# Last layer's expert rows by one-hot products on chip, and a ninth slot in the ring of expert weights with a quarter of the descriptors' scratch

## The reference, cut to what matters

```python
def swiglu(x, w_gu, w_down):
    g, u = jnp.split(x @ w_gu, 2, axis=-1)
    return (jax.nn.silu(g) * u) @ w_down

# moe_ffn(h, ...), h (N, D)
scores = jax.nn.sigmoid(jnp.dot(h, router_w, preferred_element_type=jnp.float32))
_, idx = lax.top_k(scores + router_bias.astype(jnp.float32), TOP_K)      # TOP_K = 6 of 64
gates = jnp.take_along_axis(scores, idx, axis=-1)
gates = gates / jnp.sum(gates, axis=-1, keepdims=True) * ROUTED_SCALE    # 2.5
...
y_rows = lax.map(expert_block, ...)        # swiglu(h[src], w_gu[e], w_down[e]) * gate
routed = jax.ops.segment_sum(y_rows.reshape(n_rows, d), src, num_segments=n_tok + 1)[:n_tok]
return routed + swiglu(h, shared_gu, shared_down)
```

## Time and profile before

| | us |
|---|---|
| median of three runs | 2591.6 |
| lowest and highest run | 2590.67, 2595.17 |
| span of the profiled execution | 2591.4 |
| TensorE busy in it (share) | 2249.8 (87%) |
| DVE busy | 740.5 (29%) |
| ScalarE busy | 417.0 (16%) |
| POOL busy | 311.3 (12%) |
| moved by DMA | 780.92 MB, of it 740.46 by the SP queue |

### The profile page before, as it was taken

One profiled execution on the slowest core, in us unless ns is written; L12 is line 12 of the kernel. 1 busy time (PEld: TensorE's weight loads), 2 busy tenths in 40 slices (PEclk: granted clock), 3 DMA queues, 4 the chain that ended last, 5 costly groups with the idle time before them and its releaser, 6 DMA issues. The chain is left out here.

```text
span 2591.4 us, 40524 instructions
## 1 busy us (share of the span) xinstructions
PE 2249.8 (87%) x17039; PEld 1151.1 (44%) x17039; DVE 740.5 (29%) x1653; ACT 417.0 (16%) x886; POOL 311.3 (12%) x368
## 2 busy tenths in 40 slices
PE   6999899999778797888888999898978889888887
PEld 2457644454333343434434557655433334343333
DVE  2365655371011011111115466645201101011112
ACT  2322344110000000000001333431000000000000
POOL 0007200011111111110000007100111101000000
PEclk8999999999989999999999999999998999999999
DMA  8000297279999999999988100136999999999994
GB/s 326 33 17 35 92 377 291 115 286 394 426 424 406 421 409 419 417 416 383 397 356 343 41 31 6 71 117 259 373 426 414 417 415 421 417 418 412 416 419 198
DMA packets 96345, 780.92 MB, mean 301 GB/s; under 512 B 21736, under 2 KB 22136, under 8 KB 37280
## 3 DMA queue, kind: packets, MB, share of 16 engines
q1 hardware_dynamic: 74848, 740.46, 69.7%
q0 software_dynamic: 21312, 37.81, 3.9%
HBM read 772.55 MB, written 41.29 MB: 314 GB/s over the span
## 5 line engine op out<-in xcount | busy, mean ns | idle before, releaser
L1513 PE MATMUL banks<-arena,htreg 128*32 128x384 f32 (+2 forms) x5824 | 879.4, 533 | 199.6 <-DMA arena<-in_exp_w_gu 194.3
L1513 PEld LDWEIGHTS banks<-arena,htreg 128*32 128x32 f32 (+2 forms) x5824 | 403.4, 137 | 648.7 <-issue 507.3
L1538 PE MATMUL banks<-arena,modreg 128*32 128x512 f32 (+2 forms) x2184 | 400.0, 598 | 40.5 <-issue 37.8
L2314 DVE TENSOR_TENSOR modreg<-modreg,banks 128x384 f32<-128x384 f32 x74 | 40.9, 553 | 1029.8 <-ACT modreg L1831 1029.8
L1538 PEld LDWEIGHTS banks<-arena,modreg 128*32 128x32 f32 (+2 forms) x2184 | 137.6, 127 | 250.4 <-issue 247.8
L1064 PE MATMUL banks<-arena,htreg 128*128 128x512 f32 (+3 forms) x480 | 159.0, 490 | 0.0
L2466 DVE COPY modreg<-banks 128x512 f32<-128x512 f32 x68 | 47.0, 691 | 318.9 <-PE banks L1538 318.9
L1837 ACT ACTIVATE modreg<-banks 128x384 f32<-128x384 f32 x74 | 36.3, 490 | 550.5 <-PE banks L1529 550.5
L2629 POOL DMA_INDIRECT y_d<-modreg,lst x68 | 67.5, 992 | 455.4 <-DVE modreg L2466 454.5
L1064 PEld LDWEIGHTS banks<-arena,htreg 128*128 128x128 f32 x480 | 89.7, 191 | 65.0 <-issue 61.0
L1831 ACT ACTIVATE modreg<-banks 128x384 f32<-128x384 f32 x74 | 36.3, 490 | 491.5 <-PE banks L1513 491.5
(11 more groups left out here) (407 smaller groups left out, 2173.6 us busy)
## 6 DMA issues: line engine op xcount, KB each, us to landing
arena<-in_exp_w_gu SPq DMA_DIRECT2D x256, 1536.0 KB
arena<-in_exp_w_down SPq DMA_DIRECT2D x128, 1536.0 KB
arena<-in_w_mod SPq DMA_DIRECT2D x32, 1024.0 KB, 11.4
arena<-y_d SPq DMA_DIRECT2D x6, 3072.0 KB, 16.7
modreg<-in_w_mod SPq DMA_DIRECT2D x14, 1024.0 KB, 8.3
modreg<-mod_d SPq DMA_DIRECT2D x20, 512.0 KB
arena<-in_shared_w_gu SPq DMA_DIRECT2D x6, 1536.0 KB
arena<-in_w_in SPq DMA_DIRECT2D x4, 2048.0 KB, 12.5
```

Of the source, the lines that this page charges most:

```text
L1513: last = mm(gu_bank(n, half)[rows, 0:DE], src[:, k, rows], up4[q][:, i, DE * half:DE * (half + 1)], start=(k == 0), stop=(k == KD - 1))
L1538: last = mm(ps[4 + half][rows, :], actT[:, k, rows], dn3[q][:, k, 512 * half:512 * half + 512], start=(k == 0), stop=(k == KE - 1))
L2314: tt(act_, sgb, gu_bank(n, 1)[:, 0:DE], ALU.mult).then_inc(unit_act.sem, 1)
```

## The change

The routed part of the last layer is written anew; layer 0 keeps its code but for the ring.

- `SLOTS` goes from 8 to 9 and the arena from 27648 to 30720 words; the room is that of the scratch for the software queue's descriptors, `dynamic_dma_scratch_size=4096` instead of the default of 16384 bytes for each partition. Both layers use the ninth slot.
- In layer 1 the units are 25 and not 34: 4 with one expert (128 slots), 4 of an expert with 96 and one with 32, 8 of two experts with 64 each, and 9 of four experts with 32 each ("quads"). The order is quad, whole, pair four times, then quad, big, pair four times, and a last quad. With the two shared units there are 27. The chunks are as many as before (195).
- The rows of a unit are gathered on chip: DVE makes a one-hot matrix `hot` from the token's place in the expert, and TensorE multiplies `h` by it, 16 products of 128 columns in the place of eight transposes. `h_d` is still stored.
- The rows are combined on chip: TensorE picks the gates of the unit's experts (`gate_rows`, 4 products), DVE turns them into a gated one-hot matrix (`gates_of`), TensorE multiplies it by the unit's outputs (`combine`, 4 products of 512 columns) and DVE adds the result (`added`) to `acc_last`. Nothing is scattered to `y_d` or read back; POOL has no work in the stage.
- The expert order comes from a permutation matrix and one product (`order_of_experts`) and not from eight rounds of max, and is complete when it is there.
- The output is stored in four pieces instead of two. In the last unit the modulation's gate is multiplied in ahead of the combining product.
- The overflow path of layer 1 (`more_last`) does its own listings, gathers and scatters, if it is entered.
- A table of 333 words for each partition is loaded in layer 1's mixer. Signals of the routing are put together on fewer semaphores. The cleared list in DRAM grows from 145 to 160 KB.

The diff, cut to its core:

```diff
-WHOLE = (4, 4)
-BIG = (12, 12)
+LAST = DEPTH - 1
+WHOLE = (4,) * LAST
+BIG = (12,) * LAST
-SLOTS = 8
-LIST1 = P * max(UNITS)
+SLOTS = 9
+LIST1 = P * NE
...
+def last_columns():
+    whole = [[(u, i) for i in range(4)] for u in range(4)]
+    big = [[(u, 0), (u, 1), (u, 2), (67 - u, 0)] for u in range(4, 8)]
+    pair = [[(r, 0), (r, 1), (r + 1, 0), (r + 1, 1)] for r in range(8, 24, 2)]
+    quad = [[(r + i, 0) for i in range(4)] for r in range(24, 60, 4)]
+    return whole + big + pair + quad
...
-        A_WORDS = 27648
+        A_WORDS = 30720
...
+        def last_work():
+            units = {kind: [u for u in range(N_LAST) if KIND_OF[u] == kind] for kind in range(4)}
+            order = []
+            for i, quad in enumerate(units[3]):
+                order.append(quad)
+                if i < 4:
+                    order += [units[0][i], units[2][i]]
+                elif i < 8:
+                    order += [units[1][i - 4], units[2][i]]
+            return [(u, tuple(dict.fromkeys(r for r, _ in COLUMNS[u]))) for u in order]
...
# SP
-                        if n == ROUTED_AT[l][FIRST]:
+                        if l < LAST and n == ROUTED_AT[l][FIRST]:
                             sp.wait_ge(sorted_ready.sem, sorted_ready.at(l, 2))
...
# TensorE
+                def order_of_experts():
+                    pe.wait_ge(order_made.sem, order_made.after(LAST, "perm"))
+                    mm(ps[0][0:1, P:P + N_COL], T_("index")[0:NE], perm, start=True, stop=True).then_inc(order_psum.sem, 1)
+                    pe.wait_ge(order_act.sem, order_act.after(LAST, "marks"))
+                    for j in range(2):
+                        last = mm(ps[3][:, N_COL * j:N_COL * j + N_COL], by_expert[:, P * j:P * j + P], perm, start=True, stop=True)
+                    last.then_inc(order_psum.sem, 1)
...
+                def gather_by_product(n):
+                    r = n - EARLY
...
+                    pe.wait_ge(slot_hot_ready.sem, slot_hot_ready.at(LAST, r + 1))
+                    for k in range(KD):
+                        for j in range(2):
+                            rows = h[:, 2 + j, :].rearrange("p (d k) -> p k d", k=KD)
+                            last = mm(ps[k // 4][:, tok(k % 4)], rows[:, k, :], hot[r % 2][:, j, :], start=(j == 0), stop=(j == 1))
+                    last.then_inc(slotT_psum.sem, 1)
+                def gate_rows(n):
+                    u = WORK[l][n][0]
...
+                    for i in range(4):
+                        column = perm[:, 4 * u + i:4 * u + i + 1].broadcast_to([NE, 32])
+                        last = mm(gu_bank(n, 0)[32 * i:32 * i + 32, :], column, by_expert, start=True, stop=True)
+                    last.then_inc(gate_psum.sem, 1)
...
+                def combine(n, j):
...
+                    for half in range(2):
+                        if j and n < NW[l] - 1:
+                            pe.wait_ge(comb_added.sem, comb_added.at(0, 4 * r + half + 1))
+                        mm(comb_bank(n, j, half), gated[r % 2][:, P * j:P * j + P], outs[r % 2][:, 512 * half:512 * half + 512],
+                           start=True, stop=True).then_inc(comb_psum.sem, 1)
...
+                    for n in range(EARLY, NW[l] + 1):
+                        if n < NW[l]:
+                            unit_part(n, "lo")
+                        act_transposed(n - 1)
+                        if n > EARLY:
+                            gate_rows(n - 1)
+                        if n < NW[l]:
+                            unit_part(n, "hi")
+                        if n >= EARLY + 2:
+                            combine(n - 2, 0)
+                        if n + 1 < NW[l]:
+                            gather_by_product(n + 1)
+                        if n >= EARLY + 2:
+                            combine(n - 2, 1)
+                        unit_down(n - 1)
+                    for j in range(2):
+                        combine(NW[l] - 1, j)
...
# DVE
+                    def one_hot(n):
+                        r, u = n - EARLY, WORK[l][n][0]
+                        if r >= 2:
+                            dve.wait_ge(slotT_psum.sem, slotT_psum.at(l, r - 1))
+                        tt(hot[r % 2].rearrange("p t (c s) -> p t c s", s=32), bc(places[:, :, 4 * u:4 * u + 4], 3, 32),
+                           bc(bc(K("slot_no")[:, 0:32], 1, 4), 1, 2), ALU.is_equal).then_inc(slot_hot_ready.sem, 1)
...
+                    for n in range(EARLY, NW[l] + 1):
+                        if n > EARLY:
+                            gates_of(n - 1)
+                        if n < NW[l]:
+                            unit_times(n)
+                        if n >= EARLY + 2:
+                            added(n - 2, 0)
+                        if n + 1 < NW[l]:
+                            unit_copied(n + 1)
+                        if n >= EARLY + 2:
+                            added(n - 2, 1)
+                        if n < NW[l]:
+                            unit_out(n - 1)
+                        if n + 2 < NW[l]:
+                            one_hot(n + 2)
+                        if n == EARLY:
+                            overflow_addresses()
...
-    nc = bacc.Bacc("TRN2", target_bir_lowering=False, num_devices=1)
+    nc = bacc.Bacc("TRN2", target_bir_lowering=False, num_devices=1, dynamic_dma_scratch_size=4096)
```

More of the change, by code:

```diff
@@ L369, in build @@
         RING = 4
-        eid = sb("eid", [P, NE], U32)
+        eid = sb("eid", [P, max(NE, N_COL)], U32)
         lst1 = sb("lst1", [P, max(UNITS)], U32)
@@ new lines, in _ @@
+                dve.wait_ge(h_ready.sem, h_ready.at(2 * l + 1, n_t))
+                link(dve.memset(mask[:, n_t, :], 0.0))
+                dve.wait_ge(order_act.sem, order_act.after(l, "scores"))
+                link(tt(selb[:, nt_, :], scores[:, nt_, :], bc(srow("rbias"), 1, n_t), ALU.add))
+                for i in range(n_t):
+                    link(dve.max(out=top8[:, i, :], in_=selb[:, i, :]))
+                    link(dve.max_index(out=idx8[:, i, :], in_max=top8[:, i, :], in_values=selb[:, i, :]))
```

568 lines of the change are left out of this document (395 added, 173 removed).

## The result

The kernel after takes 2536.7 us (median of four runs, 2532.6 to 2537.6) against 2593.1 (four runs) for the kernel before on the same chip: a ratio of 0.978, 95% interval 0.977 to 0.979. The forecast was 2511 us with a range of 2494 to 2536. The direction holds; that the weights' transfers bound the last layer's expert stage throughout does not, and 26 us of the 81 that were expected aren't there.

The account below looks back on a forecast made before the run. Weight transfers were taken to bound the expert stages. Last landing 2497.2, less 3 for layer 0, plus 7 for the last down product and 9.2 for the end, gave 2510.4; 0.2 more, say 2511 us; range 2494 to 2536.

Parts of the forecast that it names:

- Loads before the ring: Last layer's expert loads: first chunk at 1766.8, the SP queue's 18.0 us wait for the expert order goes, none replaces it.
- Rows and pitch: Last layer's expert stage: row traffic goes, 192 chunks at 3.77 us each take 723.8 us.
- rival 3: Expert transfers: no lag, queue at 426 GB/s, 3.70 us a chunk, 13 us less, layer 0 gains 4: 2494; chance 0.12.
- The lag of 5 us: End of the last layer's weight transfers: some DMA engines finish late; 5 us kept, ends 0 and 10.
- TensorE: Last-layer units: 25.1 us each with a 4.4 us gather; 75.4 us a group against 79.2 of weights, cover 3.8.
- Rival 1: Last layer's first groups: TensorE becomes the bound; at 6.1 us a gather 16 us more, 2527; chance 0.20.
- The ninth slot: Layer 0's ring: one more chunk held ahead of each shared unit saves 3 us, between 0 and 8.
- Rival 2: Last layer's ring: nine slots don't carry quads, the queue starves for 16 us, 2529; chance 0.12.
- The scratch: Layer 0's software-queue descriptors: a quarter of the scratch costs nothing, between 0 and rival 5's price.
- rival 5: Layer 0: small scratch makes POOL wait for the previous DMA's landing, 192 us dearer, 2703; chance 0.05.
- Rival 4: Last layer: rows were hidden, chunk pitch stays 3.87 to 4.0; at 3.96 landing 37 us later, 2548; chance 0.06.
- The end: After the last landing: 7 us for the last down product, then 9.2 for gating, combining, add, handovers and store.

Follow-up runs that it names:

- e1: Kernel after with the gather reading neighbouring words of h instead of every eighth (features mixed, same amount of work): 2499.9 us, 0.9635 of the kernel before.
- e2: Kernel after with half of the gather's products left out, stride kept: 2497.9 us, ratio 0.9635.
- e6: Kernel after, whole computation, VectorE writing the last layer's h in gather order and gate/up weights laid out to match: 2502.5 us, ratio 0.9653.
- e11: e6 plus software-queue copies on POOL, DRAM to DRAM, 128 rows of 4 KB for each of 24 last-layer units, never read: 2526.2 us, ratio 0.975.
- e12: e11 with each copy written in 256 pieces of 2048 bytes with a gap behind each, same bytes: 2524.0 us, ratio 0.975.
- e3: Kernel before with nine slots and the small descriptor scratch, one semaphore of the output's stores spared: 2583.9 us, ratio 0.9968.
- e4: Kernel before with only the small descriptor scratch (4096 bytes): 2592.7 us against 2591.8, ratio 1.0001.
- e5: Kernel after with eight ring slots instead of nine: 2574.2 us, ratio 0.992.
- e8: e6 with eight ring slots instead of nine: 2521.7 us, ratio 0.974.
- e7: Kernel after with the gather's weight loads reading every second word instead of every eighth (features mixed): 2500.2 us, ratio 0.965.
- e10: Kernel after with the gather's weight loads reading every fourth word instead of every eighth (features mixed): 2535.8 us, ratio 0.978.
- e9: Kernel after, whole computation, gather on neighbouring words, last-layer lo/hi weight chunks loaded in matching order as 3072-byte pieces: 2513.4 us, ratio 0.970.

## Why the prediction was right or wrong

The sum and what it met, in the trace of the kernel after:

| term | forecast | after |
|---|---|---|
| first expert issue | 1763.8 | 1763.05 |
| from there to the last landing | 730.4 | 751 |
| to the end of the last down product | 7 | 10 |
| end | 9.2 | 11.7 |
| sum | 2510.4 | 2535.7 |

**What bounds the kernel before** was read rightly, by the windows of share 1.00 with TensorE idle in between. e1, e2 and e6 are bound in the same way again: they stand at a DMA share of 1.00 and more.

**Loads before the ring** came true but for a wait of 2.60 us for a weight in the first unit of four: ten chunks in one run of issues from 1763.05, where the earlier trace rows has a gap until 1788.85. **Rows and pitch**: the step of 3.77 us a chunk was mis-sized, to the careful side. I took the spacing of the pairs and left the 426 GB/s that the window of the same pair shows to rival 3. Where the queue isn't starved it now moves 429 GB/s, which is 3.67 us a chunk; over e1's whole stage, with its first 300 us at 422 to 425, the mean is about 3.71 ((714.6 - 1.6) / 192). The lag of 5 us isn't there: after the last chunk the DMA share falls from 0.48 to 0.00 within 4 us. From first issue (1764.4) to last landing (some 2479: share 0.60 in 2474 to 2478, 0.09 in the next 4 us) e1 takes about 714.6 us, 16 under the forecast. This is about rival 3's time for the stage, and it would have given about 2494 + 3 + 2.5 with the end as measured, which is e1's 2500. (Rival 3's 13 us are its faster pitch alone; the 5 us of lag that it does away with are missing from its sum.) The guess of the Trainium skill, "DMA: Bandwidth & Descriptors", section "Latency and other measured facts", beside that rival was that the software queue slows two engines. In e11 and e12 that queue is in use again and the total stays at 428 to 429 GB/s, so nothing of it shows for such copies.

**TensorE** is the step that failed. Its terms for gating and combining held (0.99 and 3.54 against 0.9 and 3.45). The gather's range was 4.4 to 6.1 and it took 7.65, above the far end. That end was built as a weight load of the earlier trace rows alone with nothing overlapped, so it could only be too low if the load itself was another one, and it was: 335 ns for 190. With 28.4 us a unit, a group of quad, whole and pair takes 85.3 against 21 x 3.70 = 77.7 of weights: the cover of 3.8 us that the sum named is -7.6. The loss of 36.8 us (after against e1) would be 4.8 such groups. There are only four, 30 us; by the GB/s of the windows, after against e1, 28 us are lost from 1800 to 2100 and 9 from 2100 to 2400 (417, 416 and 416 against 429, 429 and 428). From the fifth group on a group is 24 chunks, 88 us at 3.67, against the same 85.3 of TensorE (an estimate): the weights are the longer by under 3 us, TensorE's waits come back at 2221.86, and the share still dips now and then, as in 2270 to 2280. Two of the marks that the prediction had named for being wrong are there: no wait for weights in the first groups after the one at 1796, and a DMA share under 0.95. Rival 1 was the right mechanism: TensorE is the bound in the first groups. Its place, its sign and the point from which it decides are in the trace; its price of 16 us came from a bound that was none, and that put the time just outside the range. What was said for rival 1, that no such series had been run, should have been followed to the operand.

The trace of before did hold a warning, if a weak one. The contiguous transposes load their tile in 140 ns, the strided ones in 193 and 201 (L1495 by eight words in all but the shared units, L1529 by three):

```profile
L1348 PEld LDWEIGHTS banks<-const,htreg x240: 137/140/230, 321.0 to 1714.6; 128*128 128x128 f32 x120
```

```profile
L1495 PEld LDWEIGHTS banks<-const,hreg x288: 138/193/226, 1187.4 to 2518.7; 128*128 128x128 f32 x144
```

```profile
L1529 PEld LDWEIGHTS banks<-const,modreg x222: 187/201/233, 531.9 to 2547.2; 128*128 128x128 f32 x111
```

53 to 61 ns more a load, on 32 loads, would have given 1.7 to 2.0 us on top of 4.4 to 6.1: a far end of 8.1 that holds the 7.65 (an estimate). As a central value it would still have been too low, since the product's loads grew by 145 ns. Nor did the longer record show in the time: eight transposes of L1495 take 1.0 us, 0.125 us each, beside the 0.14 of L1416.

**The ninth slot** was worth 5 to 9 us in layer 0 and not 3: 8.7 (e3 against e4) or 5.1 (e3 against before), 8.5 (after against e5), 5.0 (e6 against e8). The upper bound of 8, the bytes missing in 1180 to 1290, was the better value, though that window is hardly changed (389 for 386 GB/s): the gain lies ahead of it, 535 to 1180, at 415 and not 411. **Rival 2** (nine slots don't carry quads) falls: with e1's gather nine slots keep the share at 1.00. It would have been true of eight (e8: 15 us).

**The scratch** costs nothing, as taken; rival 5 falls (e4, and POOL's rows). **Rival 4** (rows were hidden, a pitch of 3.87 or more) falls by e1's pitch of 3.71 without rows; e11, where as many bytes cost 24 us, agrees.

**The end** was 5.5 us too short. The last down product waits for the gating and the eight combining instructions of the unit before it, not for its weights, whose landing was over by about 2514. Behind it the final combining products wait 2.04 us for the gated rows: four VectorE steps of 1.22 us (L2703, L2704) run until 2524.60, 0.6 after the product's end at 2523.98, and stand ahead of them in order. Then 5.37 us for combining where 3.45 were counted, and 3.6 for the store. The clock is part of that: the same eight instructions took 3.96 us at 2514.73, at a granted clock of 1.00, and after the 2.04 us without work they run at 0.68, in 2528 to 2530 at 0.50, the lower level of 1.2 GHz:

```profile
2526.02:2531.40 5.38, 5.37 (x8) 2.00 (x8) 2.06 (x3) 0.00 (x0) 0.00 (x0) 0.68 0.28 100
```

**The whole.** Of the 55.7 us between the two traces 33.5 lie in the last landing (2547.5 to 2514) and 22.2 in the tail behind it; the forecast had 53.3 and 27.7. The miss of 25 us in the trace is less than its largest term alone: the gather's 37 us and the end's 5.5 came on top, and transfers 16 us faster than forecast took some of it back. That the time fell so near the range is partly luck.

## What to carry to other kernels

When an operation is priced by another line's row, compare how each operand is laid out, not only the tile's shape: here the same 128 x 128 load cost 190 or 335 ns by the distance of its words, and a cover forecast at 4 us in 79 was none, which made 2537 us of 2500. Put a stride where few instructions pay for it (four VectorE instructions, 3 us) and not where many do (800 weight loads, 34 us, or 128 transfers at 2% less rate, 11 us more than on VectorE). A cover that thin deserves a forecast from its far side, or an experiment, before anything rests on it.

## What the runs showed of the hardware

- In fp32 products a weight load of 128 columns takes 192 ns from neighbouring words (e1), 196 from every second (e7), 330 from every fourth (e10) and 335 from every eighth (after); in a series of 128-column products that is 0.117, 0.123, 0.234 and 0.239 us an instruction. In transposes (before) it takes 140 ns from neighbouring words and 193 from every eighth, at 0.125 us an instruction.
- VectorE's 1024-column instructions with two fp32 inputs take 1.22 to 1.28 us on neighbouring words (after) and 1.92 to 2.01 (e6) where the output, or the output and one input, step by 128 words.
- Chunks of 1.573 MB in pieces of 12288 bytes move at 428 to 429 GB/s where nothing starves the queue (e1, e6); with two thirds of them in pieces of 3072 it is 420 (e9). Copies of 12.6 MB from DRAM to DRAM on the software queue beside them leave the rate of all traffic at 428 to 429 (e11, e12).
- A quarter of the descriptors' scratch, 4096 bytes, changes nothing for the three indirect transfers of 128 rows to a unit of layer 0: scatters issue in 992 ns and land after 9.5 us (e4) as with 16384 (992, 9.4), and the time's ratio is 1.0001.
- After 2.04 us without work at the very end TensorE's granted clock was 0.68 over 5.4 us and 0.50 within them, and eight combining instructions took 5.37 us for 3.96 at 1.00.
